# Expert gates added into a zeroed DRAM table by indirect DMAs, instead of one-hot products on TensorE

## The chip, the core and the metric

The kernel runs on one core of a Trainium2 chip. The metric is the device time of one execution in microseconds (us), given as the median of three runs. The profile comes from one further execution, whose own time and span are given below.

## The reference, cut to what matters

One layer of a network on 512 tokens of width 2048: a mixing block (an SSD branch, an HGRN2 branch, two gated products, an output product), then a feed-forward block that picks experts for each token. The change touches only the feed-forward block, and borrows idle DMA time from the HGRN2 branch.

```python
def peer_ffn(h, w_q, sub_keys, u, v):          # 512 tokens, 8 heads, 128 x 128 = 16384 experts
    q = (hf @ w_q).reshape(t, PEER_HEADS, 2, PEER_D_HALF)
    s = jnp.einsum('thpd,hpkd->thpk', q, sub_keys).astype(jnp.float32)
    s1, i1 = lax.top_k(s[:, :, 0], PEER_TOPK)  # 16 best of 128 first keys, 16 best second keys
    s2, i2 = lax.top_k(s[:, :, 1], PEER_TOPK)
    ...                                        # 16 best of the 256 sums: idx = i1 * 128 + i2
    gate = jax.nn.softmax(top_s, axis=-1)
    act = jax.nn.gelu(jnp.einsum('td,tkd->tk', xt, jnp.take(u, it, axis=0)))
    out = jnp.einsum('tk,tkd->td', gt * act, jnp.take(v, it, axis=0))
```

So each token has 8 heads times 16 experts, 128 (expert, gate) pairs. Within one head the 16 experts of a token differ; two heads can pick the same expert, and then their gates add.

## The kernel before, in words

The kernel is a chain of stages, each with its own block of programs for SP (which issues plain DMAs), POOL (which issues indirect DMAs), ACT, PE and DVE. All large products share one **ring**: SP loads a weight tile of 128 x 2048 floats (1 MB) into one of two slots of `ring.raw` (`load_tile`), ACT rounds it to `ring.high` (L190), DVE or POOL subtracts to get `ring.low` (L1933 or L195), and PE multiplies high and low parts with the high and low parts of the activations (`product`, L213 to L215: 16 steps of three matmuls, 48 per tile). Semaphores `low_ready` and `used` carry the ring: PE starts tile n when its low part is there, and a slot is loaded again when its low part has been taken.

The tokens are split. For the **first 128 tokens** ("own") the experts' rows are fetched: POOL issues 128 indirect DMAs (`fetch`, L1503; one expert row of 8 KB for each of 128 tokens), into four slots, and DVE takes the dot products (`take_dot`, L1917). For the **other 384 tokens** all 16384 experts are computed as dense products: 128 tiles `u_tiles`, each giving 128 experts times 384 tokens, through Gelu on ACT (L1699) into the DRAM tensor `gelu`. These dense results must be weighted by a dense table of gates, `gates`, that is zero nearly everywhere.

`route_stage` makes all this. First come 32 tiles in which the queries (16 tiles of `w_query`) alternate with 16 tiles of `u_tiles`, and DVE selects the best keys. Then come 112 tiles of `u_tiles`, in pairs: 3 "free" pairs, while DVE ends the selection; 24 "gate" pairs; 29 "late" pairs. In the gate pairs the table is built: for each of 384 tokens, DVE makes a one-hot matrix of the first keys times gates (`hot_rows`, L1927), ACT one of the second keys (`ones_of`, L1729 and L1733), PE multiplies them (L1830, 8 products of 128 x 128 a tile), ACT copies the results (L1747) to `gate_table`, and SP stores 12 blocks of 2 MB. In gate tiles DVE takes one dot product a tile, in late tiles three in two tiles, until all 128 are taken. In the free, gate and late tiles DVE's program is in this order: low part of the next tile, then one or two dot products, then the low part of the tile after it. DVE runs its instructions strictly in that order. POOL has the low parts of the first 38 tiles, and only then the fetches.

`output_stage` then reads `gelu` and `gates` four keys at a time (`Weights.load`, `weigh` L144), and multiplies with `v_tiles`.

Of the kernel before, what the change touches and what calls it, by code (L numbers as in the profile page):

```python
# [21 lines left out]
F32 = mybir.dt.float32  # L22
# [31 lines left out]
GT = 32  # L54
# [5 lines left out]
NEG = -3.0e38  # L60
LAG = 2
# [57 lines left out]
class Weights:  # L119
# [7 lines left out]
    def __init__(self, nc, ctx):  # L127
        with nc.sbuf_tensor("gate_table", [P, 2 * KEYS * GT], F32, side="right") as table:
            self.table = table
        sb = lambda n, s, dt=F32: ctx.enter_context(nc.sbuf_tensor(f"weights_{n}", s, dt, side="right"))[:]  # L130
        self.gelu, self.w = sb("gelu", [P, VGROUP, REST]), sb("w", [P, VGROUP, REST])
        self.gate = sb("gate", [P, REST // GT, VGROUP, GT])
        self.high0, self.low0 = sb("high0", [P, VGROUP, REST], F32R), sb("low0", [P, VGROUP, REST], F32R)

    def load(self, sp, scratch, g, landed):
# [3 lines left out]
        sp.dma_start(self.gate, scratch["gates"][:, :, ds(VGROUP * g, VGROUP)].rearrange("b i j t -> i b j t")  # L139
                     ).then_inc(landed, 16)  # L140

    def weigh(self, vec):
        by_block = lambda x: x.rearrange("p j (b t) -> p j b t", t=GT)
        return vec.tensor_tensor(by_block(self.w), by_block(self.gelu), self.gate.rearrange("p b j t -> p j b t"),  # L144
                                 ALU.mult)
# [638 lines left out]
def hg_stage(nc, dram, ring, h, const, y_out, following):  # L784
# [8 lines left out]
    with ExitStack() as ctx:  # L793
# [34 lines left out]

        consts = sem("consts")
# [24 lines left out]
        def _(sp):  # L854
# [5 lines left out]

            def store(p):
                sp.wait_ge(o_ready, p + 2)
                sp.dma_start(one(y_out[ds(p, 1)]), o_norm[:]).then_inc(o_stored, 16)

            for n in range(HG_TILES, 3 * HG_TILES):
                load_tile(sp, ring, n % 2, dram["w_hg"][n], n)
            with sp.Fori(3, H) as u:
# [5 lines left out]
            load_ahead(sp, ring, H * HG_TILES, following)  # L873
            for p in range(H - 3, H):
                store(p)
            sp.wait_ge(o_stored, 16 + 16 * H)
# [145 lines left out]
        def _(dve):  # L1022
# [7 lines left out]
            vec.memset(eps4[:], 4.0 * EPS)  # L1030

# [478 lines left out]
def route_stage(nc, dram, ring, h, x, norm_w, rstd, const, scratch, row_of, weight, weights, following):  # L1510
# [10 lines left out]
    with ExitStack() as ctx:  # L1521
# [7 lines left out]
        GROUP = 4  # L1529
        BANKS = 4  # L1530
        BLOCK_TURNS = GT // GROUP // BANKS
        GATE_PAIRS = REST // GROUP // BANKS
        BLOCKS = REST // GT
        FREE_PAIRS, EXP_AFTER = 3, 2
        SLOTS = 4
        LATE_PAIRS = PAIRS - FREE_PAIRS - GATE_PAIRS

        table = weights.table[:].rearrange("p (b j t) -> p b j t", b=2, j=KEYS)
        hot1 = sb("hot1", [P, 2, GROUP, KEYS])
        hot2 = sb("hot2", [P, 2, GROUP, KEYS])  # L1540
        far = sb("far", [P, GROUP, KEYS])
        place = sb("place", [P, 2, T])
        gate = rstd
# [8 lines left out]
        spare = weights.table[:]  # L1552
        at = [0]

        def carve(*shape):
            n = int(np.prod(shape))
            at[0] += n
            assert at[0] <= 2 * KEYS * GT
# [27 lines left out]
        exp_in, exp_done, gates_ready, turned, vec_done = (  # L1586
            sem(n) for n in ("exp_in", "exp_done", "gates_ready", "turned", "vec_done"))
        hot_ready, ones_at = sem("hot_ready"), sem("ones_at")
        distanced = sem("distanced")
        placed = sem("placed")  # L1590
        made = sem("made")
        taken = sem("taken")
        table_stored = sem("table_stored")
# [11 lines left out]
        def _(sp):  # L1605
            for half in range(2):
                a, b = slice(half * KT // 2, (half + 1) * KT // 2), slice(half * P // 2, (half + 1) * P // 2)
                sp.dma_start(keys[:, a], dram["sub_keys"][:, a]).then_inc(table_stored, 16)
                sp.dma_start(count[:, b], dram["count"][:, b]).then_inc(gelu_stored[half], 16)

# [38 lines left out]
            for i in range(FREE_PAIRS):  # L1649
                turn(i)  # L1650

            def gate_block(blk, buf):
                with sp.Fori(0, BLOCK_TURNS) as j:
                    turn(blk * BLOCK_TURNS + j + FREE_PAIRS)
# [4 lines left out]
            with sp.Fori(0, BLOCKS // 2) as b2:  # L1659
                for buf in range(2):  # L1660
                    gate_block(2 * b2 + buf, buf)
            with sp.Fori(FREE_PAIRS + GATE_PAIRS, PAIRS - 2) as i:
                turn(i)
            sp.wait_ge(table_stored, 16 * (BLOCKS + 2))
# [10 lines left out]
        def _(pool):  # L1675
# [4 lines left out]

            split_low_all(nc, pool, ring, FIRST + 2 * FREE_PAIRS)
            pool.wait_ge(own_ready, 1)
            for k in range(HK):
                fetch(k)

        @block.scalar
        def _(act):
# [34 lines left out]
            def ones_of(i, b):  # L1722

                if b == 0:
                    act.wait_ge(placed, 1)
                act.wait_ge(ones_at, BANKS * i + b)
                for g in range(GROUP):
                    t = (i * BANKS + b) * GROUP + (OWN + g)
                    ins = nc.scalar.activation(far[:, g], count[:], ACT.Abs, bias=place[:, 1, ds(t, 1)])  # L1729
                ins.then_inc(distanced, 1)  # L1730
                act.wait_ge(distanced, BANKS * i + (b + 1))
# [649 lines left out]
```

## Time and profile before

| | us |
|---|---|
| median of 3 runs | 5006.86 (5006.20 to 5008.29) |
| the profiled execution | 5005.71 |
| its span, first to last instruction | 5003.9 |
| PE busy | 4865.2 (97%) |
| DVE busy | 3167.1 (63%) |
| ACT busy | 1689.4 (34%) |
| POOL busy | 1059.0 (21%) |

The stages lie as follows in the span: start and SSD to about 735 us, HGRN2 from there to about 1635, the two mixing stages and the output product to 2556, `route_stage` from 2556 to about 3930, `output_stage` from there to the end. In `route_stage` the 3 free pairs end at about 2952, the gate pairs reach from 2952 to 3439, the late pairs follow. The profile's busy share of PE hides little idle time; what matters is how long PE takes for one tile in each of these stretches, and which engine would be next.

### The profile page before, as it was taken

The page shows a single profiled execution, that of the slowest core. Times are in us where ns is not written, and L with a number is a line of the kernel's source. Part 1 is how long each engine was busy: PE and PEld are TensorE (multiplying, and loading weights), DVE is VectorE, ACT ScalarE, POOL GpSimd, SP SyncE. Part 2 cuts the span into 40 slices and gives each one's busy share as a digit, 9 for nine tenths or more (in the row PEclk, how much of TensorE's full clock was granted, in tenths as well). Part 3 has the DMA queues.
Part 4 walks back from the last instruction along what each step waited for, and adds up shares of the span by engine and source line. Part 5 has one row for each costly group of instructions (what it writes and reads, how often), then busy time and mean ns, then how long its engine had stood idle before and what let it go on. Part 6 is the DMA issues. An engine that isn't in the chain of part 4 may idle for free. (4 is left out here: it accounts for less than half of the span.)

```text
span 5003.9 us, 65592 instructions
## 1 busy us (share of the span) xinstructions
PE 4865.2 (97%) x24160; PEld 4199.5 (84%) x24160; DVE 3167.1 (63%) x4253; ACT 1689.4 (34%) x1740; POOL 1059.0 (21%) x425
## 2 busy tenths in 40 slices
PE   8999969999999999999989999999999899999998
PEld 6777758888887787887879999999999788888887
DVE  5666658878888100101038866666767599888888
ACT  3223223333333322222232348875222222222221
POOL 2333310000000344443334430001322011111110
PEclk9999989999999999999999999999999999999999
DMA  3222212222221333334323357778998799888885
GB/s 123 80 84 88 80 59 87 80 80 80 82 80 65 128 113 113 141 126 166 114 92 116 113 213 281 277 279 305 336 341 327 278 338 319 307 305 308 299 300 204
DMA packets 238757, 913.95 MB, mean 183 GB/s; under 512 B 18400, under 2 KB 109152, under 8 KB 160608
## 3 DMA queue, kind: packets, MB, share of 16 engines
q1 hardware_dynamic: 201824, 644.63, 36.6%
q0 software_dynamic: 36864, 268.45, 14.7%
q8 instruction: 37, 0.61, 0.1%
q14 instruction: 32, 0.26, 0.0%
HBM read 837.78 MB, written 75.24 MB: 182 GB/s over the span
## 5 line engine op out<-in xcount | busy, mean ns | idle before, releaser
L195 POOL TENSOR_TENSOR ring_low<-ring_raw,ring_high 128x2048 fp32r<-128x2048 f32 x165 | 767.5, 4652 | 2181.9 <-ACT ring_high L190 2181.9
L213 PE MATMUL rt_acc<-h_high,ring_high 128*128 128x384 f32 (+1 forms) x2304 | 792.1, 344 | 15.0 <-DVE h_low L231 12.3
L214 PE MATMUL rt_acc<-h_low,ring_high 128*128 128x384 f32 (+1 forms) x2304 | 785.7, 341 | 0.0
L215 PE MATMUL rt_acc<-h_high,ring_low 128*128 128x384 f32 (+1 forms) x2304 | 785.4, 341 | 0.0
L190 ACT ACTIVATE ring_high<-ring_raw 128x2048 fp32r<-128x2048 f32 x336 | 643.6, 1916 | 380.5 <-PE out_acc L215 127.8
L213 PEld LDWEIGHTS rt_acc<-h_high,ring_high 128*128 128x128 f32 x2304 | 433.6, 188 | 30.2 <-issue 9.8
L215 PEld LDWEIGHTS rt_acc<-h_high,ring_low 128*128 128x128 f32 x2304 | 433.4, 188 | 10.5
L214 PEld LDWEIGHTS rt_acc<-h_low,ring_high 128*128 128x128 f32 x2304 | 433.6, 188 | 9.3
L213 PE MATMUL hg_acc<-h_high,ring_high 128*128 128x512 f32 x1024 | 408.3, 399 | 9.6 <-DVEq L1025 9.6
L215 PE MATMUL hg_acc<-h_high,ring_low 128*128 128x512 f32 x1024 | 401.1, 392 | 0.0
L214 PE MATMUL hg_acc<-h_low,ring_high 128*128 128x512 f32 x1024 | 399.7, 390 | 0.0
L1933 DVE TENSOR_TENSOR ring_low<-ring_raw,ring_high 128x2048 fp32r<-128x2048 f32 x106 | 243.0, 2293 | 227.6 <-ACT ring_high L190 227.6
L1503 POOL DMA_INDIRECT x_mid_front<-u_rows,row_of x128 | 169.9, 1327 | 743.0 <-DVE sb_rt_dot L1917 725.3
L1503 POOL DMA_INDIRECT sb_op_rows<-v_tiles,row_of x128 | 121.4, 948 | 941.0 <-DVE x_tok_back L2122 848.8
L213 PE MATMUL ssd_acc<-h_high,ring_high 128*128 128x512 f32 x768 | 305.7, 398 | 9.9 <-DVE h_low L231 6.3
L215 PE MATMUL ssd_acc<-h_high,ring_low 128*128 128x512 f32 x768 | 300.8, 392 | 0.0
L214 PE MATMUL ssd_acc<-h_low,ring_high 128*128 128x512 f32 x768 | 300.6, 391 | 0.0
L2122 DVE SCALAR_TENSOR_TENSOR x_tok_back<-sb_op_rows,own_weight,x_tok_back 128x2048 f32<-128x2048 f32 x128 | 300.2, 2346 | 0.0
L1917 DVE CUSTOM_DVE_ANT_0 x_mid_front<-x_mid_front,sb_rt_h_tok 128x2048 f32<-128x2048 f32 x128 | 292.7, 2286 | 0.0
L2146 DVE TENSOR_TENSOR x_tok_back<-x_tok_back,op_out 128x512 f32<-128x512 f32 x384 | 261.1, 682 | 45.5 <-PE op_out L2104 42.6
L2057 ACT ACTIVATE sb_op_more_high<-ring_raw 128x2048 fp32r<-128x2048 f32 x64 | 120.3, 1912 | 375.5 <-PE op_out L2104 333.4
L213 PEld LDWEIGHTS hg_acc<-h_high,ring_high 128*128 128x128 f32 x1024 | 193.1, 189 | 48.5 <-issue 11.1
(319 smaller groups left out, 9950.6 us busy)
## 6 DMA issues: line engine op xcount, KB each, us to landing
ring_raw<-u_tiles SPq DMA_DIRECT2D x128, 1024.0 KB, 5.5
ring_raw<-v_tiles SPq DMA_DIRECT2D x128, 1024.0 KB, 6.6
ring_raw<-w_hg SPq DMA_DIRECT2D x64, 1024.0 KB, 4.8
ring_raw<-w_ssd SPq DMA_DIRECT2D x48, 1024.0 KB, 4.7
ring_raw<-w_mix_s SPq DMA_DIRECT2D x32, 1024.0 KB, 4.8
ring_raw<-w_mix_h SPq DMA_DIRECT2D x32, 1024.0 KB, 4.8
gelu<-sb_rt_gelu SPq DMA_DIRECT2D x128, 192.0 KB, 5.1
gates<-gate_table SPq DMA_DIRECT2D x12, 2048.0 KB, 7.7
```

The lines of the kernel that those rows point to most:

```text
L190: nc.scalar.activation(ring.high[:, slot], ring.raw[:, slot], ACT.Copy).then_inc(ring.high_ready, 1)
L195: nc.gpsimd.tensor_tensor(ring.low[:, slot], ring.raw[:, slot], ring.high[:, slot].bitcast(F32), ALU.subtract).then_inc(ring.low_ready, 1)
L213: nc.tensor.matmul(out, high[:, m], x_high[:, k, tokens], start=(k == 0), stop=False, skip_group_check=True)
L214: nc.tensor.matmul(out, high[:, m], x_low[:, k, tokens], start=False, stop=False, skip_group_check=True)
L215: last = nc.tensor.matmul(out, low[:, m], x_high[:, k, tokens], start=False, stop=(k == KT - 1), skip_group_check=True)
L1503: return pool.indirect_dma_start(rows[0:OWN, slot], None, table, bass.IndirectOffsetOnAxis(ap=row_of[0:OWN, k:k + 1], axis=0))
L1917: vec.tensor_tensor_reduce(rows[0:OWN, slot], rows[0:OWN, slot], h_tok[0:OWN], 1.0, 0.0, ALU.mult, ALU.add, dot[0:OWN, slot:slot + 1]).the ...
L1933: vec.tensor_tensor(ring.low[:, slot], ring.raw[:, slot], ring.high[:, slot].bitcast(F32), ALU.subtract).then_inc(ring.low_ready, 1)
L2057: nc.scalar.activation(v_high[s], ring.raw[:, s % 2], ACT.Copy).then_inc(ring.high_ready, 1)
L2122: vec.scalar_tensor_tensor(x_tok[0:OWN, 0], rows[0:OWN, slot], weight[0:OWN, ds(k, 1)], x_tok[0:OWN, 0], ALU.mult, ALU.add).then_inc(summe ...
L2146: vec.tensor_tensor(x, x, ps_out[(2 * OUTS * buf + OUTS * half + i) % BANKS][:], ALU.add).then_inc(out_added, 1)
```

## The change

The table of gates is laid out anew, as `gates[i, j, t]` (first key, second key, token), 128 x 128 x 384 floats or 25.2 MB. It is set to zero in the HGRN2 stage: 16 plain DMAs of 1.57 MB from a tile of zeros, issued by SP between the weight loads. In `route_stage` DVE computes for each of 384 tokens and 128 (head, k) the address of its entry, and POOL issues 384 indirect DMAs, each of which adds 128 gates (one per partition, 4 bytes) into the table. Four of them stand behind each of the first 96 fetches. All 48 DMAs of a head share a semaphore, and the next head's first one waits for it. One-hot matrices, their products, copies and stores are gone, and so are the 12 transposes ahead of them (L1819). The 106 tiles behind the free pairs now all have the late tiles' form; DVE takes four dot products in three tiles.

```diff
@@ Weights
-        self.gate = sb("gate", [P, REST // GT, VGROUP, GT])
+        self.gate = sb("gate", [P, VGROUP, REST])
...
-        return vec.tensor_tensor(by_block(self.w), by_block(self.gelu), self.gate.rearrange("p b j t -> p j b t"), ...
+        return vec.tensor_tensor(self.w, self.gelu, self.gate, ALU.mult)
@@ hg_stage, SP
+            def zero(u):
+                sp.dma_start(runs[:, ds(RUNS * u, RUNS)], zeros[:].unsqueeze(1).to_broadcast([P, RUNS, T])
+                             ).then_inc(zeroed, 16)
...
                     if s == 1:
                         store(u - 3)
+                    if s == 2:
+                        zero(u - 1)
@@ route_stage, SP
-                sp.wait_ge(taken, blk * (GT // GROUP) + (GT // GROUP + BANKS))
-                sp.dma_start(scratch["gates"][ds(blk, 1)].rearrange("b i j t -> (b i) j t"),
-                             table[:, buf]).then_inc(table_stored, 16)
...
+            for done in scattered:
+                sp.wait_ge(done, 16 * TOPK * (NC - 1))
@@ route_stage, POOL
+            def scatter(e):
+                head, c, k = e // (TOPK * (NC - 1)), e // TOPK % (NC - 1), e % TOPK
+                at = slice(head * TOPK + k, head * TOPK + k + 1)
+                if e % (TOPK * (NC - 1)) == 0 and head > 0:
+                    pool.wait_ge(scattered[head - 1], 16 * TOPK * (NC - 1))
+                pool.indirect_dma_start(scratch["gates"].rearrange("i j (t a) -> (i j t) a", a=1),
+                                        bass.IndirectOffsetOnAxis(ap=gate_at[:, c, at], axis=0), gate[:, c, at], None,
+                                        compute_op=ALU.add).then_inc(scattered[head], 16)
...
             for k in range(HK):
                 fetch(k)
+                for e in range(min(entries, SCATTERS * k), min(entries, SCATTERS * (k + 1))):
+                    scatter(e)
@@ route_stage, ACT: ones_of and gate_block removed
-                nc.scalar.activation(hot2[:, b % 2], far[:], ACT.Relu, bias=const["ones"][:, 0:1],
-                                     scale=-1.0).then_inc(ones_at, 1)
@@ route_stage, PE
-                        for g in range(GROUP):
-                            last = nc.tensor.matmul(ps_gate[b][:, g * KEYS:(g + 1) * KEYS], hot1[:, b % 2, g],
-                                                    hot2[:, b % 2, g], start=True, stop=True)
@@ route_stage, DVE
+            vec.tensor_copy(gate[:], rest(best))
+            chain.after(vec.scalar_tensor_tensor(at_gate[:], rest(chosen[:, 0]), float(KEYS), rest(chosen[:, 1]),
+                                                 ALU.mult, ALU.add))
...
+            vec.tensor_copy(gate_at[:], at_gate[:]).then_inc(scatter_ready, 1)
...
-                    hot_rows(2 * i + q, 0)
...
+            for j in range(RUN):
...
+                low(first + j, (j + 1) % 2)
...
+                for k in range(dots_at(j), dots_at(j + 1)):
                     take_dot(k, k % SLOTS, k // SLOTS)
```

**POOL, behind its last low parts.** Before, the fetches (`u_rows` into `x_mid_front`) follow each other, each with a wait for a free slot:

```order
L195 TENSOR_TENSOR ring_low<-ring_raw,ring_high 128x2048
L194 REGISTER_ALU
L195 TENSOR_TENSOR ring_low<-ring_raw,ring_high 128x2048
L201 REGISTER_ALU
L201 COMPARE_AND_BRANCH
L1503 DMA x_mid_front<-u_rows,row_of 128x2048 x128
```

Now four additions into `gates` stand between two fetches (the names of the semaphores waited for are in brackets):

```order
L1518 DMA x_mid_front<-u_rows,row_of 128x2048 [waits rt_dotted,rt_scatter_ready,rt_own_ready]
L1682 DMA gates<-sb_rt_gate,sb_rt_gate_at 6291456x1 x4
L1518 DMA x_mid_front<-u_rows,row_of 128x2048 [waits rt_dotted]
L1682 DMA gates<-sb_rt_gate,sb_rt_gate_at 6291456x1 x4
...
L1518 DMA x_mid_front<-u_rows,row_of 128x2048 [waits rt_dotted]
L1682 DMA gates<-sb_rt_gate,sb_rt_gate_at 6291456x1 [waits rt_scattered0]
L1682 DMA gates<-sb_rt_gate,sb_rt_gate_at 6291456x1 x3
L1518 DMA x_mid_front<-u_rows,row_of 128x2048 [waits rt_dotted]
```

A fetch is now every fifth instruction of POOL for the first 96 fetches, and every twelfth group of additions begins with a wait for the head before.

**DVE, from the end of the selection to the first dot products.** Before, three copies out of PSUM, and then in each gate tile eight one-hot rows ahead of the low part:

```order
L1909 COPY sb_rt_place<-rt_gate 128x512
L1910 TENSOR_SCALAR sb_rt_place<-rt_gate 128x512
L1911 COPY ffn_rstd<-rt_gate 128x512
...
L1927 TENSOR_SCALAR sb_rt_hot<-sb_rt_count,sb_rt_place,ffn_rstd 128x128
L1932 ISA
L1933 TENSOR_TENSOR ring_low<-ring_raw,ring_high 128x2048
L1915 ISA
L1916 REGISTER_ALU
L1917 ISA x_mid_front,sb_rt_dot<-x_mid_front,sb_rt_h_tok 128x2048
```

Now the addresses are computed, and low parts and dot products follow each other:

```order
L1865 COPY sb_rt_gate<-routing 128x384
L1866 SCALAR_TENSOR_TENSOR sb_rt_at_gate<-routing 128x384
L1870 TENSOR_SCALAR sb_rt_at_gate<-sb_rt_at_gate,sb_rt_rest_at 128x128 x3
L1873 CAST sb_rt_gate_at<-sb_rt_at_gate 128x384
L1887 TENSOR_TENSOR ring_low<-ring_raw,ring_high 128x2048
L1879 ISA x_mid_front,sb_rt_dot<-x_mid_front,sb_rt_h_tok 128x2048
L1879 ISA sb_rt_dot 128x1
L1882 COPY sb_rt_dots<-sb_rt_dot 128x1
L1887 TENSOR_TENSOR ring_low<-ring_raw,ring_high 128x2048
```

Nothing stands any more between the low parts and the dot products; the next low part is behind the dot product, and with it behind the fetch that the dot product waits for.

**SP, in the loop over the heads of the HGRN2 stage.** Now a DMA of zeros stands behind the third weight load; before, the loads and the store of `y_hg` stood alone:

```order
L169 DMA ring_raw<-w_hg 128x2048
L865 ISA
L865 DMA gates<-sb_hg_zeros 128x6x512
L165 REGISTER_ALU
L169 ISA
L169 DMA ring_raw<-w_hg 128x2048
```

The next weight load is behind the zeros on the same queue, and it has its own wait for a free slot.

## Rows read from the trace of the kernel before

**Rows 1.** Stretches: busy us (instructions) of each engine, granted clock, DMA share, GB/s.

```profile
2934.55:3447.07 512.52, 511.81 (x3230) 511.46 (x3229) 339.45 (x589) 401.92 (x682) 58.79 (x55) 1.00 0.77 280
3439.70:3740.00 300.30, 300.30 (x1734) 300.30 (x1733) 211.16 (x198) 84.77 (x74) 86.57 (x53) 1.00 0.91 340
```

**Rows 2.** ACT timeline, Gelu of a tile: start, duration, what, idle time before it.

```profile
2934.55 0.49 ACT L1699 ACTIVATE sb_rt_gelu<-rt_acc 128x384 f32<-128x384 f32 x1 [6.02 <-PE rt_acc L215]
...
3447.07 0.49 ACT L1699 ACTIVATE sb_rt_gelu<-rt_acc 128x384 f32<-128x384 f32 x1 [5.45 <-PE rt_acc L215]
...
3729.94 0.49 ACT L1699 ACTIVATE sb_rt_gelu<-rt_acc 128x384 f32<-128x384 f32 x1 [6.08 <-PE rt_acc L215]
```

**Rows 3.** Waits from 3440 to 3740: who, for whom, total, times, longest.

```profile
ACT sb_rt_gelu L1699 <- PE rt_acc L215: 215.5, 36, 6.1
POOL x_mid_front L1503 <- DVE sb_rt_dot L1917: 211.0, 36, 9.1
DVE ring_low L1933 <- ACT ring_high L190: 90.0, 36, 5.3
```

**Rows 4.** POOL timeline, the first fetches.

```profile
2951.41 0.94 POOL L1503 DMA_INDIRECT x_mid_front<-u_rows,row_of  x1 [0.30 <-issue]
2952.65 0.93 POOL L1503 DMA_INDIRECT x_mid_front<-u_rows,row_of  x1 [0.30 <-issue]
```

**Rows 5.** POOL timeline, two fetches of a late pair.

```profile
3487.45 2.99 POOL L1503 DMA_INDIRECT x_mid_front<-u_rows,row_of  x1 [7.43 <-DVE sb_rt_dot L1917]
3490.74 0.94 POOL L1503 DMA_INDIRECT x_mid_front<-u_rows,row_of  x1 [0.30 <-issue]
```

**Rows 6.** DVE timeline over the same time.

```profile
3487.33 2.29 DVE L1917 CUSTOM_DVE_ANT_0 x_mid_front<-x_mid_front,sb_rt_h_tok 128x2048 f32<-128x2048 f32 x1
...
3490.94 2.29 DVE L1933 TENSOR_TENSOR ring_low<-ring_raw,ring_high 128x2048 fp32r<-128x2048 f32 x1 [1.12 <-ACT ring_high L190]
3493.14 2.28 DVE L1917 CUSTOM_DVE_ANT_0 x_mid_front<-x_mid_front,sb_rt_h_tok 128x2048 f32<-128x2048 f32 x1
```

**Rows 7.** DVE timeline at the start of `output_stage`.

```profile
3946.40 1.75 DVE L144 TENSOR_TENSOR weights_w<-weights_gelu,weights_gate 128x1536 f32<-128x1536 f32 x1
```

**Rows 8.** POOL timeline there.

```profile
3946.68 2.29 POOL L1503 DMA_INDIRECT sb_op_rows<-v_tiles,row_of  x1 [0.31 <-issue]
```

**Rows 9.** All fetches of `route_stage`: duration in ns min/median/max, first and last start.

```profile
L1503 POOL DMA_INDIRECT x_mid_front<-u_rows,row_of x128: 932/938/2998, 2950.0 to 3861.8; - x128
```

**Rows 10.** DMA queues from 3440 to 3740: packets, MB, share of 16 engines.

```profile
q0 software_dynamic: 7577, 55.13, 49.9%
q1 hardware_dynamic: 10567, 46.97, 41.2%
...
x_mid_front<-u_rows,row_of POOLq DMA_INDIRECT x53, 8.0
```

**Rows 11.** DMA issues of the whole span: count, KB each, us to landing.

```profile
ring_raw<-w_hg SPq DMA_DIRECT2D x64, 1024.0 KB, 4.8
gates<-gate_table SPq DMA_DIRECT2D x12, 2048.0 KB, 7.7
sb_hg_norm_w<-hg_norm_w SPq DMA_DIRECT2D x1, 0.5 KB, 3.1
...
sb_ssd_norm_w<-ssd_norm_w SPq DMA_DIRECT2D x1, 8.0 KB, 1.9
```

**Rows 12.** SP's waits from 820 to 1650, the HGRN2 stage.

```profile
SPq L171 <- DVE ring_low L1047: 726.5, 56, 19.2
```

**Rows 13.** A stretch at the end of SSD, columns as in rows 1.

```profile
695.00:750.00 55.00, 32.28 (x133) 23.80 (x133) 18.77 (x38) 14.56 (x17) 0.00 (x0) 0.72 0.18 58
```

**Rows 14.** PE's waits from 690 to 750.

```profile
PE ssd_ps_y L538 <- DVE sb_ssd_c_dec L702: 12.5, 4, 3.2
```

More of the change, by code:

```diff
@@ L60 @@
 NEG = -3.0e38
+SCATTERS = 4
 LAG = 2
@@ L138, in load @@
                      ).then_inc(landed, 16)
-        sp.dma_start(self.gate, scratch["gates"][:, :, ds(VGROUP * g, VGROUP)].rearrange("b i j t -> i b j t")
-                     ).then_inc(landed, 16)
+        sp.dma_start(self.gate, scratch["gates"][:, ds(VGROUP * g, VGROUP)]).then_inc(landed, 16)
     def weigh(self, vec):
-        by_block = lambda x: x.rearrange("p j (b t) -> p j b t", t=GT)
-        return vec.tensor_tensor(by_block(self.w), by_block(self.gelu), self.gate.rearrange("p b j t -> p j b t"),
-                                 ALU.mult)
+        return vec.tensor_tensor(self.w, self.gelu, self.gate, ALU.mult)
 class Ring:
@@ L778, in ssd_stage, with hg_stage @@
     ring.base += G * SSD_TILES
-def hg_stage(nc, dram, ring, h, const, y_out, following):
+def hg_stage(nc, dram, ring, h, const, y_out, gates, following):
     H = HG_HEADS
@@ L827, in hg_stage @@
         ps_k = ps("ps_k", [P, T])
+        zeros = sb("zeros", [P, T])
+        zeros_made, zeroed = sem("zeros_made"), sem("zeroed")
         consts = sem("consts")
@@ L1030, in _ @@
             vec.memset(eps4[:], 4.0 * EPS)
+            vec.memset(zeros[:], 0.0).then_inc(zeros_made, 1)
             dve.wait_ge(consts, 32)
@@ L1528, in route_stage @@
         PAIRS = (KEYS - BEFORE) // 2
-        GROUP = 4
         BANKS = 4
-        BLOCK_TURNS = GT // GROUP // BANKS
-        GATE_PAIRS = REST // GROUP // BANKS
-        BLOCKS = REST // GT
         FREE_PAIRS, EXP_AFTER = 3, 2
         SLOTS = 4
[L1536 to L1543, printed above, removed]
+        RUN = 2 * (PAIRS - FREE_PAIRS)
+        dots_at = lambda j: min(HK, 4 * j // 3)
+        at_gate = sb("at_gate", [P, NC - 1, HK])
+        gate_at = sb("gate_at", [P, NC - 1, HK], U32)
+        gate = sb("gate", [P, NC - 1, HK])
+        rest_at = sb("rest_at", [P, NC - 1])
         gelu = sb("gelu", [P, 2, REST])
@@ L1550, in route_stage @@
         dots = sb("dots", [P, HK])
-        spare = weights.table[:]
+        spare = weights.routing[:]
         at = [0]
@@ L1907, in _ @@
             chain.after(vec.tensor_copy(weight[0:OWN], best[0:OWN, 0].rearrange("p h k -> p (h k)")))
-            dve.wait_ge(turned, 1)
-            vec.tensor_copy(place[:, 0], ps_gate[0][:])
-            vec.tensor_scalar(place[:, 1], ps_gate[1][:], -1.0, None, ALU.mult).then_inc(placed, 1)
-            chain.after(vec.tensor_copy(gate[:], ps_gate[2][:]))
+            rest = lambda x: x[:, 1:NC].rearrange("p c h k -> p c (h k)")
+            vec.tensor_copy(gate[:], rest(best))
+            chain.after(vec.scalar_tensor_tensor(at_gate[:], rest(chosen[:, 0]), float(KEYS), rest(chosen[:, 1]),
+                                                 ALU.mult, ALU.add))
+            dve.wait_ge(rest_landed, 16)
+            for c in range(NC - 1):
+                ins = vec.tensor_scalar(at_gate[:, c], at_gate[:, c], float(REST), rest_at[:, c:c + 1],
+                                        ALU.mult, ALU.add)
+            chain.after(ins)
+            vec.tensor_copy(gate_at[:], at_gate[:]).then_inc(scatter_ready, 1)
             def take_dot(k, slot, turn):
@@ L1920, in take_dot @@
                 vec.tensor_copy(dots[0:OWN, ds(k, 1)], dot[0:OWN, slot:slot + 1]).then_inc(dot_kept, 1)
-            def hot_rows(i, b):
-                dve.wait_ge(made, BANKS * i + (b + 3))
-                for g in range(GROUP):
-                    t = (i * BANKS + b) * GROUP + (OWN + g)
-                    ins = vec.tensor_scalar(hot1[:, b % 2, g], count[:], place[:, 0, ds(t, 1)], gate[:, ds(t, 1)],
-                                            ALU.is_equal, ALU.mult)
-                ins.then_inc(hot_ready, 1)
             def low(n, slot):
@@ L2271 @@
     "ident": [P, P], "ones": [P, P], "later": [P, P], "upto": [P, P], "level_mask": [P, LEVELS + 1, P],
-    "count": [P, P],
+    "count": [P, P], "rest_at": [P, NC - 1],
 }
```

120 lines of the change are left out of this document (29 added, 91 removed).

## The prediction, written before the changed kernel ran

> **What bounds the kernel now.** I read the busy line of the page first: PE is busy for 97% of the span, and POOL, which the change loads, for only 21%. The 40 slices show DMA shares of 5 to 9 tenths from the middle of `route_stage` on. Then I cut that stage into stretches. In the gate pairs and in the late pairs PE and its weight loads fill the whole stretch at full granted clock, and DMA has a share of 0.77 and 0.91 [rows 1]. The time of a tile is the distance between two Gelu instructions on ACT [rows 2]: from the one at 3447.07 to the one at 3729.94 there are 34 tiles, so 282.87 / 34 = 8.32 us a tile in the late pairs; from 2934.55 to 3447.07 there are 51 (2 free tiles, 48 gate tiles and the first late one), so 512.52 / 51 = 10.05 us on average. ACT, DVE and POOL wait, in the end, for PE: ACT 215.5 us for PE's products, DVE 90.0 us for ACT, POOL 211.0 us for DVE's dot products, and PE is in no row of the waits of that stretch [rows 3]. So PE is the bound, and a tile without gate products costs 8.32 us as long as nothing else takes longer.
>
> **What goes away.** At 8.32 us a tile the 51 tiles take 424.3 us, against 512.5: the one-hot products, the transposes and the small stalls around them cost 88.2 us, and all of it is on PE. The work of ACT and DVE on the one-hot matrices lay beside PE and gives nothing of its own. The 12 stores of 2 MB go too; PE did not wait for them. So PE alone would give -88 us.
>
> **What is added for nothing, or nearly.** The zeros: 16 DMAs of 1.57 MB. A store of 2 MB landed in 7.7 us [rows 11], so 1.57 MB takes about 5.8 us. SP waits 726.5 us in 56 waits for free slots in the HGRN2 stage, 13 us each [rows 12], and a load needs 4.8 us [rows 11]; the load behind the zeros is issued when they have landed. Cost 0; without that cover at most 16 x 5.8 = 93 us. The memset of the zeros, the copy and the address arithmetic on DVE: seven instructions of up to 384 columns, at a time when PE has tiles in the ring and POOL is still at its last low part; about as long as the three copies they replace. I take 0 and at most 3 us. The gates read by `weigh` are now contiguous; DVE's instruction and PE do not get shorter by it, so 0.
>
> **What POOL now has to do.** A fetch takes 0.94 us on POOL, and with the 0.30 us up to the next one the spacing is 1.24 us (2951.41 to 2952.65) [rows 4]. The trace shows no addition into DRAM. The nearest row is the fetch: it too is one indirect DMA with 128 addresses out of SBUF, so I take 1.24 us; I bound it from below by 0.62 us, half of that, since it names as many places as a fetch but moves 4 bytes at each, and from above by the 2.99 us of rows 5. For one dot product POOL now issues 1 + 4 instructions, 5 x 1.24 = 6.20 us. DVE wants four dot products in three tiles, so PE's pace gives 8.32 x 3/4 = 6.24 us. Without any other loss POOL would be just fast enough, with 0.04 us to spare. That is the place that decides.
>
> **The loss that is there.** Of the 128 fetches some took 2.99 us [rows 5, 9]. The timelines tell why: the fetch began at 3487.45, 0.12 us after DVE had begun a dot product (2.29 us, both inputs in SBUF), and ended at 3490.44, 0.8 us after that had ended [rows 5, 6]. It stood still until DVE's instruction was over, and then did its work. The same with a plain two-input instruction: DVE's `weigh` ran from 3946.40 to 3948.15, the fetch that began at 3946.68 took 2.29 us, to 3948.97 [rows 7, 8]. A fetch in a gap is not slowed by what follows: the one at 3490.74 was 0.20 us old when the low part began at 3490.94, and took 0.94 us [rows 5, 6]. So an indirect DMA needs something that DVE holds only at its very start; it must find the start of its work outside of DVE's two-input instructions.
>
> The Trainium skill says this in "SBUF — State Buffer", in the section on who interferes with whom: a DVE instruction with two SBUF inputs contends with a GpSimd instruction that reads SBUF. By that rule the trace agrees for 2.99 us against 0.94 us. The same section infers that `tensor_tensor` doesn't hold up descriptor generation, since that needs the write side; here the trace, with 2.29 us under `weigh`, decides against the inference.
>
> Now the count for three tiles: DVE runs three low parts and four dot products, 7 x 2.29 = 16.0 us, and POOL has 20 instructions. Before, a fetch was issued just when DVE had ended, so nearly all were free of this; now POOL issues without a pause and meets every DVE instruction. A DVE instruction that stands alone costs POOL 2.29 us, less the part of a POOL instruction already under way (on average 0.62 us), less some 0.1: about 1.6 us. A low part with a dot product directly behind it (3490.94, 3493.14 [rows 6]) costs 2 x 2.29 - 0.7 = 3.8 us if POOL gets nothing in between, and 1.6 + (2.28 - 1.15) = 2.7 us if it gets its turn between them, which no row shows. With three such pairs and one more dot product that meets POOL after its turn (1.1 us), three tiles cost POOL 24.8 + 3 x 2.7 + 1.1 = 34.0 us or 24.8 + 3 x 3.8 + 1.1 = 37.3 us; I take the middle, 35.7 us, 11.9 us a tile. PE needs 24.96 us.
>
> What is behind it: DVE's dot product waits for the fetch, the next low part stands behind the dot product, and PE waits for the low part. The four slots only shift this by some microseconds, as POOL has no lead to build up. 96 dot products carry additions, 72 tiles: 72 x (11.9 - 8.32) = 257.8 us. Seven times POOL also waits for the last addition of a head; it was issued one fetch (1.24 us) before, and a small DMA lands in 1.9 to 3.1 us [rows 11]: I take 2 us, together 14 us; up to 8 us each, the landing of a fetch [rows 10], 56 us. The last 34 tiles run at 8.32 us as before.
>
> DMA time. The late pairs use 49.9% for 1.5 fetches a tile and 41.2% for the rest [rows 10]: 4.15 us and 3.43 us. With 4/3 fetches that is 3.69 + 3.43 = 7.1 us in a tile of 11.9, so 4.8 us are left for 5.33 additions. Each has 8 gates for each of the 16 engines. That suffices if an addition takes less than 0.9 us of each engine. No row shows one; a DMA of 128 single floats landed in 3.1 us with two others before it [rows 11], which is the upper bound if nothing overlaps; the lower bound is nothing.
>
> PE's clock. PE will idle about 3.6 us a tile, most of it where two dot products stand between two low parts. Where PE had four waits of up to 3.2 us within 55 us the granted clock was 0.72 on average [rows 13, 14], so it will fall to 1.2 GHz now and then. A tile at 1.2 GHz all along would take 16.6 us. But PE has 35.7 us for what it does in 24.96 us at full clock, so it can run at half clock for 21 of them and still not be late: I take 0, at most 72 x (16.6 - 11.9) = 338 us.
>
> **The sum.** 5005.7 - 88.2 + 257.8 + 14 = 5189. The profiled run, 5005.7, is within 1.2 us of the median of the runs, 5006.9, so the sum stands for the median as well: 5190 us. With 34.0 and 37.3 us for three tiles it is 5149 and 5228.
>
> **Rivals.**
> - *POOL keeps up; faster.* If the additions do not stop at DVE's instructions, or are so much cheaper on POOL that their spacing is under about 0.6 us (25.0 less 4 x 1.24 for the fetches and some 10.8 for DVE's instructions, over 16), PE stays the bound: 5005.7 - 88.2, and 14 us at most from the heads, 4918 to 4932 us. Against it: fetch and addition alike read 128 addresses out of SBUF, and not only dot products stopped a fetch. For it: no row shows an addition. It turns to the other side at a gain of 88 us used up: 88 / 72 = 1.2 us a tile, that is when three tiles cost POOL 28.6 us instead of 25. Chance 0.09.
> - *The additions are slow in the DMA engines.* Reading and writing single floats in DRAM one after the other, the queue would hold up the fetches behind them. With y us of each engine per addition, three tiles take 21.3 + 16 y us; at 1.5 us that is 45.3, so 24 x (45.3 - 25.0) = 487 and 5405 us; at 3.1 us it is 70.9, 24 x 45.9 = 1102 and 6020 us. The trace would show landings of the fetches far over 8 us and a DMA share near 1. Chance 0.15.
> - *PE falls to 1.2 GHz and stays there.* It would need 16.6 us a tile and be the bound: 72 x 8.3 = 598, 5515 us. Against it: PE at 1.2 GHz is busy, and in the trace it has never stayed down beside busy tiles. Chance 0.05.
> - *No change.* Gain and loss could cancel in a narrow band only. Chance 0.03.
> - The forecast, POOL as the bound: 0.68. Its own range reaches from 5120 (additions a little cheaper, 0.2 us less each: 384 x 0.2 = 77) to 5310 (0.3 us dearer, 115 us).
>
> **How the numbers follow.** A difference of 0.2% is about what a measurement of this kernel can tell from none. Faster 0.09, the same 0.03, slower 0.88. The range leaves out the faster case (0.09) and the slower half of the slow additions (about 0.08); it is 5080 to 5450.
>
> **What would show it.** Right: POOL busy nearly without a pause from 2950 for some 860 us, with many of its indirect DMAs at 1.5 to 3 us; DVE waiting for DMA (`u_rows` landing) at the dot products; PE waiting for DVE's low parts, tiles 11 to 13 us apart for the first 72 and 8.32 us for the last; the granted clock below 1 there; the HGRN2 stage unchanged within 2 us. Wrong: tiles at 8.32 us from the start (then the additions are not stopped); POOL waiting and fetches landing in 15 us or more (then the DMA engines); additions of 0.94 us throughout in spite of DVE; a longer HGRN2 stage.

## The result: 6.8% slower

| | before | after |
|---|---|---|
| median, us | 5006.53 (5005.99 to 5008.29, 4 runs) | 5343.28 (5341.79 to 5348.32, 4 runs) |
| ratio, 95% interval | | 1.0676 (1.0663 to 1.0689) |
| profiled execution, us | 5005.71 | 5344.22 |
| its span, us | 5003.9 | 5342.4 |

The kernel lost 337 us. The time lies in the range (5080 to 5450) and on the side that was forecast, but 153 us above the forecast of 5190, and above the 5120 to 5310 that the prediction gave for its own main case: the loss is 1.8 times the 184 us foreseen.

**The page of after.** The busy line, share of the span and instructions of each engine:

```profile
PE 4855.8 (91%) x23380; PEld 4176.4 (78%) x23380; DVE 3069.4 (57%) x3873; ACT 1411.3 (26%) x1164; POOL 1817.4 (34%) x809
```

PE is no longer busy for 97% of the span; POOL went from 1059.0 to 1817.4 us. The slices of the span show where:

```profile
PE   8999979999998999999899766666669999999998
...
POOL 2333300000003444433344888888872011111110
PEclk9999979999999999999999888888889999999999
DMA  3222223333333333343233666666668599888885
```

The columns are the slices of the span, 134 us each. In slices 23 to 30 PE falls to 6 or 7 tenths, POOL stands at 8 (at last 7), the granted clock at 8 tenths and DMA at 6. PE slower and DMA less loaded at once: something else sets the pace there.

**Stretches**, columns as in [rows 1]; the first is the time of the additions, the second the tiles behind them and the start of `output_stage`, the third the HGRN2 stage:

```profile
2952.20:3978.30 1026.10, 683.41 (x3511) 668.62 (x3510) 395.63 (x361) 173.74 (x148) 879.89 (x480) 0.83 0.64 187
3978.30:4260.00 281.70, 277.12 (x1584) 276.49 (x1584) 155.89 (x133) 77.25 (x67) 48.96 (x32) 0.99 0.74 271
735.00:1640.00 905.00, 892.31 (x4606) 754.75 (x4606) 726.52 (x1033) 305.16 (x263) 4.59 (x1) 0.99 0.33 110
```

In the first stretch POOL has 480 instructions, 96 fetches and 384 additions, and with the 0.30 us in front of each it is never free: 879.9 + 144 = 1024 of 1026.1 us. PE is busy for 683 of them, where it was busy for all in [rows 1]. In the HGRN2 stage PE's 892.31 us stand against 892.30 in the same stretch of before; the zeros raised the DMA share from 0.24 to 0.33 and cost nothing.

**The tiles**, on ACT's timeline, as in [rows 2] (start, duration, what, idle time before it):

```profile
3306.96 0.49 ACT L1708 ACTIVATE sb_rt_gelu<-rt_acc 128x384 f32<-128x384 f32 x1 [19.89 <-PE rt_acc L213]
...
3318.06 0.49 ACT L1708 ACTIVATE sb_rt_gelu<-rt_acc 128x384 f32<-128x384 f32 x1 [8.62 <-PE rt_acc L213]
...
3326.30 0.49 ACT L1708 ACTIVATE sb_rt_gelu<-rt_acc 128x384 f32<-128x384 f32 x1 [5.93 <-PE rt_acc L213]
...
3348.79 0.49 ACT L1708 ACTIVATE sb_rt_gelu<-rt_acc 128x384 f32<-128x384 f32 x1 [20.00 <-PE rt_acc L213]
```

Three tiles take 41.83 us, as 11.10, 8.24 and 22.49 us. In each group of three one has two dot products between its low parts, and it takes 22 us; one runs at PE's own pace. The forecast said tiles 11 to 13 us apart and 35.7 us for three; the mean over the stretch is 1026.1 / 72 = 14.25 us a tile, 42.8 for three. Behind the last addition tiles come at 8.32 us again.

**Who waits**, in the first stretch, as in [rows 3] (who, for whom, total, times, longest):

```profile
ACT sb_rt_gelu L1708 <- PE rt_acc L213: 845.8, 74, 22.9
DVE x_mid_front L1879 <- DMA x_mid_front<-u_rows,row_of: 621.0, 96, 9.2
...
PE rt_acc L211 <- DVE ring_low L1887: 331.3, 46, 13.9
POOL gates L1682 <- issue: 117.0, 384, 0.3
POOL x_mid_front L1518 <- issue: 28.9, 95, 0.3
```

In [rows 3] PE was in no row and POOL waited 211.0 us for DVE. Now the chain runs the other way: PE waits for low parts (331 us), DVE for fetched rows in front of its dot products (621 us), and POOL for nothing but its own spacing. That is the chain that was foreseen.

**What POOL does**, its lines in that stretch (busy us, mean ns of one, idle time before them), and then the durations of the additions, ns min/median/max as in [rows 9]:

```profile
L1682 POOL DMA_INDIRECT gates<-sb_rt_gate,sb_rt_gate_at x384 | 724.9, 1888 | 117.0 <-issue 117.0
L1518 POOL DMA_INDIRECT x_mid_front<-u_rows,row_of x97 | 156.5, 1614 | 30.4 <-issue 29.2 <-DVE sb_rt_gate_at L1873 1.1
```

```profile
L1682 POOL DMA_INDIRECT gates<-sb_rt_gate,sb_rt_gate_at x384: 1556/1562/3662, 2953.6 to 3975.6; - x192
```

The shortest addition takes 1.56 us on POOL. It is not the fetch's 0.94 us [rows 4] that the forecast used, and this is the main miss. (A fetch that meets nothing takes 1.00 us in this stretch.)

**The stalls**, on POOL's and on DVE's timeline over the same 10 us, as in [rows 5] and [rows 6]:

```profile
3396.42 1.56 POOL L1682 DMA_INDIRECT gates<-sb_rt_gate,sb_rt_gate_at  x1 [0.31 <-issue]
3398.29 3.31 POOL L1682 DMA_INDIRECT gates<-sb_rt_gate,sb_rt_gate_at  x1 [0.30 <-issue]
3401.90 2.09 POOL L1682 DMA_INDIRECT gates<-sb_rt_gate,sb_rt_gate_at  x1 [0.30 <-issue]
3404.29 1.00 POOL L1518 DMA_INDIRECT x_mid_front<-u_rows,row_of  x1 [0.30 <-issue]
```

```profile
3397.87 2.29 DVE L1879 CUSTOM_DVE_ANT_0 x_mid_front<-x_mid_front,sb_rt_h_tok 128x2048 f32<-128x2048 f32 x1 [3.21 <-DMA x_mid_front<-u_rows,row_of]
...
3400.28 2.28 DVE L1887 TENSOR_TENSOR ring_low<-ring_raw,ring_high 128x2048 fp32r<-128x2048 f32 x1
```

The addition begun at 3398.29 met a dot product that was 0.42 us old, and took 3.31 us instead of 1.56. It ended at 3401.60, while the low part (from 3400.28 to 3402.56) was already running: so it got its turn in the moment between DVE's two instructions. The next one, begun at 3401.90 under the low part, took 2.09 us. All rows of the stretch are like these. Each of its 96 dot products and 72 of its 73 low parts held up exactly one of POOL's DMAs, and that DMA ended a fixed time after the DVE instruction: 1.42 to 1.47 us for an addition, 0.87 to 0.89 for a fetch. 70 of the 96 dot products had a low part directly behind, and each time the waiting DMA got in between.

**The DMA engines** in that stretch (queue: packets, MB, share of 16 engines; issues: count, us to landing), as in [rows 10]:

```profile
q0 software_dynamic: 68976, 100.89, 38.2%
q1 hardware_dynamic: 21024, 90.91, 25.7%
...
gates<-sb_rt_gate,sb_rt_gate_at POOLq DMA_INDIRECT x384, 4.5
x_mid_front<-u_rows,row_of POOLq DMA_INDIRECT x96, 7.2
```

The queues take 38% and 26% where they took 50% and 41%, and a fetch lands in 7.2 us against 8.0. So it isn't the DMA engines that hold the fetches up. For the zeros the same view of the whole span says:

```profile
gates<-sb_hg_zeros SPq DMA_DIRECT2D x16, 1536.0 KB, 9.7
```

They landed in 9.7 us each, not the 5.8 of the forecast; the load behind them had that much time.

### The profile page after: what moved, and what is told of

It reads as the page before. It is cut to its first block and busy times, and to the rows that moved or that the text cites. A ratio compares the mean times of both kernels' runs of the same rounds, so it can differ in the third digit from the quotient of the medians.

```text
span 5342.4 us, 61852 instructions
## 1 busy us (share of the span) xinstructions
PE 4855.8 (91%) x23380; PEld 4176.4 (78%) x23380; DVE 3069.4 (57%) x3873; ACT 1411.3 (26%) x1164; POOL 1817.4 (34%) x809
## 3 DMA queue, kind: packets, MB, share of 16 engines
q0 software_dynamic: 92160, 268.67, 15.8%
## 5 line engine op out<-in xcount | busy, mean ns | idle before, releaser
L211 PE MATMUL rt_acc<-h_high,ring_high 128*128 128x384 f32 (+1 forms) x2304 | 822.6, 357 | 360.5 <-DVE ring_low L1887 345.9
L212 PE MATMUL rt_acc<-h_low,ring_high 128*128 128x384 f32 (+1 forms) x2304 | 812.4, 353 | 0.0
L213 PE MATMUL rt_acc<-h_high,ring_low 128*128 128x384 f32 (+1 forms) x2304 | 811.6, 352 | 0.0
L1682 POOL DMA_INDIRECT gates<-sb_rt_gate,sb_rt_gate_at x384 | 724.9, 1888 | 117.0 <-issue 117.0
L211 PEld LDWEIGHTS rt_acc<-h_high,ring_high 128*128 128x128 f32 x2304 | 455.3, 198 | 390.6 <-issue 366.8
L212 PEld LDWEIGHTS rt_acc<-h_low,ring_high 128*128 128x128 f32 x2304 | 455.0, 197 | 9.3
L213 PEld LDWEIGHTS rt_acc<-h_high,ring_low 128*128 128x128 f32 x2304 | 453.6, 197 | 10.5
L1708 ACT ACTIVATE sb_rt_gelu<-rt_acc 128x384 f32<-128x384 f32 x128 | 62.9, 491 | 1128.7 <-PE rt_acc L213 1128.6
L1518 POOL DMA_INDIRECT x_mid_front<-u_rows,row_of x128 | 204.0, 1593 | 156.8 <-DVE sb_rt_dot L1879 123.4
```

What stands on the lines that cost most here:

```text
L211: nc.tensor.matmul(out, high[:, m], x_high[:, k, tokens], start=(k == 0), stop=False, skip_group_check=True)
L212: nc.tensor.matmul(out, high[:, m], x_low[:, k, tokens], start=False, stop=False, skip_group_check=True)
L213: last = nc.tensor.matmul(out, low[:, m], x_high[:, k, tokens], start=False, stop=(k == KT - 1), skip_group_check=True)
L1518: return pool.indirect_dma_start(rows[0:OWN, slot], None, table, bass.IndirectOffsetOnAxis(ap=row_of[0:OWN, k:k + 1], axis=0))
L1682: pool.indirect_dma_start(scratch["gates"].rearrange("i j (t a) -> (i j t) a", a=1), bass.IndirectOffsetOnAxis(ap=gate_at[:, c, at], axis= ...
```

## The experiments

The ratios are against the kernel before, run again beside each experiment (medians 5005 to 5009 us).

The theory: POOL is the bound for 1026 us, by the additions' own time and by the stalls under DVE's two-input instructions. The rivals: PE or the clock is slower for another reason; the DMA engines hold the fetches up; the gain of 88 us was never there.

**Additions left out.** The table stays zero, so the output of the experts lacks the weighted sums of 384 tokens; all else is as after.

```diff
-            for done in scattered:
-                sp.wait_ge(done, 16 * TOPK * (NC - 1))
...
-                for e in range(min(entries, SCATTERS * k), min(entries, SCATTERS * (k + 1))):
-                    scatter(e)
```

> The changed kernel without the 384 additions (the table of gates stays zero, so the other tokens' experts are left out of the output); zeros, addresses and the order on DVE stay. Theory A (POOL's 480 indirect DMAs take 1026 us where 96 dot products have 599, and that is all of the loss): the tiles go back to 8.32 us, 5007 - 88 = 4918 us, at most 4932. Rival B (part of the loss is elsewhere: zeros, the new order of DVE, table reads): it stays above 4940.

Measured: 4919.39 us (4918.43 to 4920.99), ratio 0.9822 (0.9806 to 0.9839). The stretch at which after lost its time (columns as in [rows 1]):

```profile
2960.00:3400.00 440.00, 440.00 (x2540) 440.00 (x2539) 287.98 (x264) 124.70 (x106) 100.45 (x70) 1.00 0.88 322
```

PE is busy without a gap at full granted clock, with a DMA share of 0.88. So the gain is there (88 us foreseen, 89 measured), and the whole loss, 5343 - 4919 = 424 us, comes with the additions. It is POOL's 1026 us less the 599 us that 72 tiles take at 8.32: 427 us.

**Plain writes in place of additions.** The same DMAs without the sum; where two heads of a token meet, the later gate stays.

```diff
-                                        bass.IndirectOffsetOnAxis(ap=gate_at[:, c, at], axis=0), gate[:, c, at], None,
-                                        compute_op=ALU.add).then_inc(scattered[head], 16)
+                                        bass.IndirectOffsetOnAxis(ap=gate_at[:, c, at], axis=0), gate[:, c, at], None).then_inc(scattered[head], 16)
```

> The changed kernel with the 384 indirect DMAs as plain writes, without the addition in the DMA engines (gates that meet in one entry are not summed). Theory A: an addition costs POOL 1.56 us because each place needs one descriptor more than a fetch; a plain write then costs 1.0 us like a fetch, POOL's stretch falls by 384 x 0.56 = 215 us, partly given back as stalls, and the time is 5130 to 5160. Rival C (1.56 us is the price of 4-byte places in DRAM, added or not): 1.56 us stays on POOL, 5344.

Measured: 5142.70 us (5142.11 to 5143.58), ratio 1.0269 (1.0251 to 1.0286). Durations of the writes, ns min/median/max:

```profile
L1682 POOL DMA_INDIRECT gates<-sb_rt_gate,sb_rt_gate_at x384: 965/981/3049, 2949.9 to 3775.2; - x192
```

A plain write of 128 single floats costs POOL 0.97 us, a fetch of 128 rows of 8 KB about the same, an addition 1.56. Bytes do not set the price; that the floats are added costs another 0.59 us on POOL. 384 x 0.59 = 227 us; 200.6 us came off, because the stalls grew, from 183 us in after to 212. With plain writes, which on POOL are nearly as cheap as the forecast took the additions to be, the kernel is still slower than before.

The expectation gave as the reason "one descriptor more" for each place. That isn't shown. The DMA packets can be counted, over the whole span, in the kernel without additions, with plain writes, and in after:

```profile
q0 software_dynamic: 36864, 268.45, 14.9%
q0 software_dynamic: 49152, 268.67, 14.7%
q0 software_dynamic: 92160, 268.67, 15.8%
```

A plain write of 128 floats leaves (49152 - 36864) / 384 = 32 packets, an addition of the same 128 floats (92160 - 36864) / 384 = 144. But a fetch leaves 144 too (36864 for 256 fetches), and costs POOL 0.94 us. So the packets don't explain the 0.59 us either, and its cause stays open.

**Three additions a fetch in place of four.** The same 384 additions lie behind 128 fetches.

```diff
-SCATTERS = 4
+SCATTERS = 3
```

> Three additions behind each of the 128 fetches instead of four behind 96. Theory A: POOL has the same 384 x 1.86 us and 32 fetches more, with their stalls, before the last addition: 128 x 1.3 + 384 x 1.86 + 128 x 1.32 + 96 x 0.76 = 1123 us, but only 10 tiles come behind that instead of 34: 1123 + 83 against 1026 + 283, 103 us less, about 5241. Rival D (the slow thing is PE's clock after each gap, not POOL's time): the gaps are as frequent, and the time is within 30 us of 5343.

Measured: 5238.57 us (5227.85 to 5240.69), ratio 1.0461 (1.0443 to 1.0478). 105 us came off with the same 384 additions. In after, the last 34 tiles ran with POOL nearly idle; now 24 of them share the load. PE's waits for low parts in the longer stretch:

```profile
PE rt_acc L211 <- DVE ring_low L1887: 215.9, 60, 6.4
```

These 216 us in 60 waits stand against 331 us in 46. So the gaps became more and the kernel faster: the rival by which PE's clock after each gap is what costs is out. A load that is the bound must be spread over all the time that it has.

**Dot products that read one input from PSUM.** The 128 tokens' activations stay in four PSUM banks, and are not copied into SBUF.

```diff
-        h_tok = sb("h_tok", [P, D])
...
+        h_tok = ps("h_tok", [P, BANKS * T])
+        ps_gate = [h_tok[:, i * T:(i + 1) * T] for i in range(BANKS)]
```

> The dot products read the tokens from PSUM, where TensorE left them, and not from a copy in SBUF; they then have one input in SBUF. Theory A with the stall at a DVE instruction's two SBUF inputs: the 97 stalls under dot products (128 us of POOL) go, the 73 under low parts (55 us) stay or grow a little: 5343 - 128 = 5215, up to 5240. Rival E (a stall comes from any long DVE instruction): no stall goes, 5343, or more if the dot product is slower from PSUM.

Measured: 5240.17 us (5231.73 to 5242.48), ratio 1.0458 (1.0441 to 1.0476). POOL's timeline and DVE's:

```profile
3199.71 1.56 POOL L1682 DMA_INDIRECT gates<-sb_rt_gate,sb_rt_gate_at  x1 [0.30 <-issue]
...
3219.71 1.56 POOL L1682 DMA_INDIRECT gates<-sb_rt_gate,sb_rt_gate_at  x1 [0.30 <-issue]
3221.57 2.62 POOL L1518 DMA_INDIRECT x_mid_front<-u_rows,row_of  x1 [0.30 <-issue]
```

```profile
3199.42 2.29 DVE L1877 CUSTOM_DVE_ANT_0 x_mid_front<-x_mid_front,rt_h_tok 128x2048 f32<-128x2048 f32 x1 [1.45 <-DMA x_mid_front<-u_rows,row_of]
...
3218.63 2.29 DVE L1877 CUSTOM_DVE_ANT_0 x_mid_front<-x_mid_front,rt_h_tok 128x2048 f32<-128x2048 f32 x1 [4.08 <-DMA x_mid_front<-u_rows,row_of]
...
3221.03 2.28 DVE L1885 TENSOR_TENSOR ring_low<-ring_raw,ring_high 128x2048 fp32r<-128x2048 f32 x1
```

The additions begun at 3199.71 and at 3219.71, each under a dot product, took 1.56 us; the fetch begun at 3221.57 under a low part, with both inputs in SBUF, took 2.62 us. The dot product itself takes 2.29 us as before. No POOL instruction was held up under a dot product any more: of 141 that began under one, none took over 0.04 us more than undisturbed. For after I put down each POOL row's time over 1.56 us (1.00 for a fetch) to the DVE instruction that ran when it began: 128 us in 96 rows under dot products, 55 us in 72 under low parts (the counts in the expectation take in two fetches behind the last addition). The 128 us are gone here, and the 55 us have become 78 in again 72 rows. 128 - 23 = 105, and 103 us came off the kernel. So the stall hangs on where DVE reads: a dot product with both inputs in SBUF holds POOL's indirect DMAs up, the same dot product with one of them in PSUM does not.

**Both together.**

> Both edits on the changed kernel: three additions behind each of 128 fetches, and the tokens read from PSUM by the dot products. Theory A, in which POOL's own time, stalls and the tiles behind the last addition add up: 128 x 1.3 + 384 x 1.86 + 96 x 1.15 (stalls under low parts) = 991 us and 83 us for the 10 last tiles, against 1026 + 283: 5343 - 235 = 5108 us. If the two gains overlapped, as where both only moved the same waits, it would stay near 5200.

Measured: 5125.40 us (5119.42 to 5126.44), ratio 1.0236 (1.0221 to 1.0252). The two gains (105 and 103) add up to 208, and 218 us came off. Even so the kernel is slower than before: POOL's own time, 128 x 1.30 + 384 x 1.86 = 881 us, is more than the 799 us of the 96 tiles beside it, and the low parts still hold it up.

**One block of 128 tokens by additions, the other 256 as before.** This starts from the kernel before. With `ADDED = 1` a third of the gate pairs becomes late pairs, and one addition stands behind each fetch; 8.4 MB are zeroed in the HGRN2 stage.

```diff
+            for e in range(ADDED * k, ADDED * (k + 1)):
+                scatter(e)
...
-        GATE_PAIRS = REST // GROUP // BANKS
+        MADE = REST - ADDED * CH
+        GATE_PAIRS = MADE // GROUP // BANKS
```

> The kernel before, with the gates of only the last 128 tokens added by indirect DMAs (128 additions, one behind each fetch, into 4 zeroed blocks) and those of the other 256 tokens still made by one-hot products: 16 gate pairs instead of 24, four dot products in three late tiles. Theory A: POOL needs 1.31 + 1.86 us and about 2 us of stalls for a dot product, less than the 6.24 us that it has, so PE stays the bound and 16 tiles fall from 10.11 to 8.32 us: 5007 - 29 = 4978 us. Rival F (any addition beside the fetches delays them, whatever POOL's load): a third of the loss per addition stays, 5007 - 29 + 142 = 5120.

Measured: 4981.20 us (4978.28 to 4982.80, 5 runs), ratio 0.9946 (0.9933 to 0.9960). That is 26 us, near a third of 88, where 29 were expected; POOL still waited 418.5 us for dot products, so it had room.

**Two blocks by additions** (`ADDED = 2`; four dot products in three late tiles).

> The same with 256 tokens' gates added, two additions behind each fetch, and 128 tokens' made by products: 8 gate pairs. Theory A: POOL needs 1.31 + 3.72 + 1.94 = 6.97 us for a dot product where the 90 late tiles give 6.24: 112 dot products lose 0.73 us each, 82 us, against a gain of 57: 5007 + 25 = 5032 us; with fewer stalls at the longer spacing, down to 4975. If only the own time of the DMAs counted (5.03 us, no stalls), 4950.

Measured: 4987.46 us (4981.47 to 4990.80), ratio 0.9960 (0.9944 to 0.9975). Waits from 2950 to 3900 (who, for whom, total, times, longest):

```profile
DVE x_mid_front L1965 <- DMA x_mid_front<-u_rows,row_of: 184.0, 56, 5.8
...
POOL x_mid_front L1517 <- DVE sb_rt_dot L1965: 68.8, 15, 5.8
...
PE rt_acc L214 <- DVE ring_low L1981: 25.6, 18, 3.2
...
POOL gates L1714 <- DMA gates<-ffn_rstd,sb_rt_place: 10.3, 7, 2.3
```

About 20 us were gained and not the 59 of two thirds. The middle of the expectation, 5032 us, had reckoned 1.94 us of stalls for a dot product; from 3120 to 3900 us they were 1.62, and the time lies near its lower edge of 4975. In the second half of the late tiles PE waits, and every third tile takes 9 to 13 us: POOL had next to no lead left.

One row near the start of this trace, on POOL's and on DVE's timeline, doesn't fit the rule of the others:

```profile
2956.31 5.96 POOL L1714 DMA_INDIRECT gates<-ffn_rstd,sb_rt_place  x1 [0.31 <-issue]
```

```profile
2956.32 2.28 DVE L1981 TENSOR_TENSOR ring_low<-ring_raw,ring_high 128x2048 fp32r<-128x2048 f32 x1
2958.53 2.28 DVE L1965 CUSTOM_DVE_ANT_0 x_mid_front<-x_mid_front,sb_rt_h_tok 128x2048 f32<-128x2048 f32 x1
```

This addition began 0.01 us ahead of the low part, was held up by it all the same, and did not get in before the dot product either. The kernel of the next experiment has one such row too, at 2961.61, 0.03 us ahead. 87 other DMAs of this trace, held up by an instruction with another directly behind it, got in between the two.

**Two blocks, dot products drawn out** over more tiles (five in four late tiles).

```diff
+                done, following_dots = (min(HK, dots_from + 5 * j // 4), min(HK, dots_from + 5 * (j + 1) // 4))
```

> As with two blocks added, but the late tiles take five dot products in four tiles instead of four in three, so POOL has 8.32 x 4/5 = 6.66 us for a dot product instead of 6.24. Theory A: POOL's time for one (1.31 + 3.72 us and about 1.5 us of stalls) now fits, the waits of PE for low parts (25.6 us before) go, 32 gate tiles at 10.11 us are saved against the kernel before: 5007 - 57 = 4950 us, up to 4965 as the last additions come only some four tiles before their table is read. Rival G (the gain of two blocks is eaten by something that does not hang on POOL's pace): it stays at 4987.

Measured: 4963.89 us (4959.73 to 4968.39), ratio 0.9912 (0.9895 to 0.9929): the fastest kernel of the study, 41 us under before. Waits from 2950 to 3960:

```profile
POOL x_mid_front L1517 <- DVE sb_rt_dot L1965: 86.1, 29, 5.4
...
POOL gates L1714 <- DMA gates<-ffn_rstd,sb_rt_place: 13.3, 6, 3.6
...
PE rt_acc L214 <- DVE ring_low L1981: 10.6, 1, 10.6
ACT weights_high L1794 <- DVE weights_w L145: 12.6, 1, 12.6
```

PE waits for a low part once, 10.6 us at the end, where `weigh` waits 10.1 us for the table to be read; that read stands behind the last additions. Up to there the tiles alternate between 8.2 and 8.4 us, and the last two take 16.3 and 13.6 us. These 13 us are most of what is missing to the 57 us expected. So the gain of two blocks did hang on POOL's pace.

## Why the prediction was right in kind and too low

- **What bounds, and what goes away:** right. PE's 8.32 us a tile and the 88 us came out in e1_no_adds to within 2 us (4919.4 against 5005.7 - 88.2 = 4917.5).
- **The zeros, the addresses, the gates' new layout:** right, nothing measurable (HGRN2 stretch 892.31 against 892.30 us).
- **"I take 1.24 us" for an addition:** this step failed. It took the fetch as the nearest row for a kind of DMA that no row showed. Measured are 1.56 + 0.30 = 1.86 us. POOL's own time is then 96 x (1.00 + 0.30) + 384 x 1.86 = 839 us and not 480 x 1.24 = 595: +244. The plain write (0.97 us) shows that the fetch was a sound stand-in for a write, and that adding has its own price on POOL. The bounds named (0.62 to 2.99) held it, but "0.3 us dearer" as the edge of the likeliest case was half of what came.
- **The stalls:** the mechanism is right, shown by e4_dots_from_psum, and the size was too high: 24 x 10.9 = 262 us forecast, 1026 - 839 = 187 measured as the rest of the stretch (183 if the rows' own excess is added up), -75. POOL met every DVE instruction, seven in three tiles, as the forecast said, but each meeting cost less. Two readings stood side by side for two DVE instructions in a row; POOL gets its turn between them, as at 3401.60, so the cheaper one holds. It gives 24 x 9.2 = 221 us, and the plain writes, whose spacing is near the forecast's 1.24 us, lost 212. The additions lost still less because of the first miss: half of a spacing of 1.86 us instead of 1.24 is over, on average, before the next DMA can meet DVE (2.29 - 0.93 - 0.1 = 1.26 us; the dot products cost 128 / 96 = 1.33 each). The order was also another than foreseen: a low part stood directly behind a dot product, which had waited for its fetch, and never a dot product directly behind a low part.
- **Waits between the heads:** 14 us forecast, none measured. At a head's border POOL's spacing stays at 0.30 us:

```profile
3079.57 2.49 POOL L1682 DMA_INDIRECT gates<-sb_rt_gate,sb_rt_gate_at  x1 [0.30 <-issue]
3082.36 1.54 POOL L1518 DMA_INDIRECT x_mid_front<-u_rows,row_of  x1 [0.30 <-issue]
3084.21 1.58 POOL L1682 DMA_INDIRECT gates<-sb_rt_gate,sb_rt_gate_at  x1 [0.30 <-issue]
```

  From the start of a head's last addition to the next head's first 4.4 to 4.9 us passed at all seven borders (here 3079.57 to 3084.21), and an addition lands in 4.5 us: it was just enough. In the kernels with one or two blocks, where the DMA share was 0.87 to 0.90 and an addition landed in 5.4 or 5.8 us, the waits do show: 17.8, 10.3 and 13.3 us.
- **The sum:** 5189 + 244 - 75 - 14 = 5344, against 5344.2 profiled. It closes because the -75 is taken as what is left of the stretch; with the 183 us of the rows it gives 5340. Two errors of opposite sign stand in it, so part of the nearness is luck: with the stalls and waits as they were and the addition at 1.24 us, the forecast would have been 5100.
- **The clock:** it fell to 0.83 and cost nothing of its own, as foreseen, and it did not stay down: behind the last addition it is 0.99, with tiles at 8.32 us. The loss over e1_no_adds (424 us) is POOL's time alone (427 us).
- **DMA engines as the bound:** refuted by a share of 0.64 and fetches that land in 7.2 us. The shares of q0 (15.8% of 5342 us in after, 14.9% of 4918 without additions) give an estimate of (844 - 733) / 384 = 0.3 us of each engine for an addition, where 0.9 would have fitted. **POOL keeps up** is refuted by e2_plain_writes too: even with a spacing of about 1.28 us for a write the kernel is slower than before.

What stays open: why DVE's read of two SBUF inputs holds an indirect DMA up at its start only; why an addition costs POOL 0.59 us more than a write; and the two additions of 5.96 us.

## What to carry to other kernels

Work that is moved to an idle engine must be priced by instructions there, not by bytes: 384 DMAs of 512 bytes cost POOL 714 us, and the 72 tiles beside which they were put last 599 us at PE's pace, of which the fetches need a fifth. Where an operation has no row, work out the pace at which the other engine would become the bound (here 0.6 us) and leave room for it to be dearer than its nearest relative: here it cost half as much again, 1.86 against 1.24 us. A replacement that doesn't fit whole can fit in part: two thirds of it, spread thinly, turned +6.8% into -0.9%.

## What the runs showed of the hardware

- An indirect DMA of 128 places costs POOL 0.93 to 1.01 us as a fetch, 0.97 us as a write of single floats and 1.56 us as an addition, and 0.30 us pass before the next. On the DMA queue the three leave 144, 32 and 144 packets.
- It is held up when DVE, at its start, runs an instruction with two inputs in SBUF (a dot product or a low part), up to the end of that instruction: all 168 times in the first stretch of after, ending 1.42 to 1.47 us behind it as an addition and 0.87 to 0.89 as a fetch. With one input in PSUM it is not (1.56 us at 3199.71). DVE's instructions keep their 2.28 to 2.29 us.
- Between two instructions of DVE, one directly behind the other, POOL gets in (3398.29 to 3401.60), 70 times of 70 in after. Two additions that began 0.01 and 0.03 us ahead of a pair did not, and took 5.96 us (at 2956.31 with two blocks by additions, at 2961.61 with them drawn out).
- Additions of 128 floats landed in 4.5 us at a DMA share of 0.64, and in 5.4 us at 0.87 (one block by additions); fetches between them in 7.2 and 7.3 us.
